# Expert weights of a two-block decoder loaded in runs of 16,384 bytes, one expert a unit, two units multiplied together

## The chip, the cores and the metric

The kernel is one program on one core of a Trainium2 chip. The metric is the device time of one execution in microseconds. Everything is float32; the matrix products of the experts run on TensorE as plain float32 matmuls. All weights come from HBM by DMAs that SyncE (SP) issues on one queue, and they pass through a ring of buffers in SBUF.

## The reference

Two blocks are computed one after the other on 256 tokens of width 1024. The first has two layers of a mixer (attention) and an expert-choice FFN; the second has one layer of another mixer and a hierarchical MoE. The change touches only how the weights of the two expert networks are fetched and multiplied:

```python
def expert_choice_ffn(h, w_router, w_gate, w_up, w_down):     # first block: 16 experts, D_EXPERT 1024
    cap = CAPACITY_FACTOR * S // N_EXPERTS                    # 32 tokens an expert
    aff = jax.nn.softmax(jnp.einsum('bsd,de->bse', h, w_router).astype(jnp.float32), axis=-1)
    gate, idx = lax.top_k(jnp.swapaxes(aff, 1, 2), cap)
    xe = h[bidx, idx]
    a = jnp.einsum('becd,edf->becf', xe, w_gate)
    u = jnp.einsum('becd,edf->becf', xe, w_up)
    ye = jnp.einsum('becf,efd->becd', jax.nn.silu(a) * u, w_down)
    return jnp.zeros_like(h).at[bidx, idx].add(gate[..., None].astype(h.dtype) * ye)

# second block: 4 groups of 8 experts, D_EXPERT_2 512, the two best of a group for each token
    hid = (jax.nn.silu(jnp.einsum('td,edf->tef', t, w_gate[gi]))
           * jnp.einsum('td,edf->tef', t, w_up[gi]) * combine[:, gi, :, None])
    out = out + jnp.einsum('tef,efd->td', hid, w_down[gi])
```

## The kernel before, in words

**Tiles and units.** Four experts (`TILE_E`) with 32 token slots each make one tile of 128 slots. The first block has two layers of four tiles, the second block eight tiles of experts of half the width. The weights of a tile come in units of 2 MB (128 partitions x 4096 float32, `UNIT`). A tile of the first block has 24 units: 8 of w_gate, 8 of w_up, 8 of w_down. A tile of the second block has 12: 4, 4 and 4. A unit holds the same rows of all four experts of the tile: for the first block row chunk c (128 rows of 1024), partition p taking row 128c+p of each expert, so that each partition gets four runs of 4096 bytes. In the second block partition p takes two rows of 512 of the eight rows 8p to 8p+7, again four runs of 4096 bytes. That makes 288 expert units in all, 604 MB of the 747 MB that are loaded.

**Buffers.** `RING` is 6 buffers; the first tile of each layer also uses four `spare` buffers in the arena (`FIRST_SLOTS`: units 0 to 11 go to buffers 9, 8, 7, 0, 1, 2, 3, 6, 4, 5, 9, 8; from unit 12 on the ring alone turns). So units 0 to 9 are loaded before the tile begins, unit 10 waits for unit 0 and unit 12 for unit 3. The second block has nine buffers in turn (`AHEAD2`), and unit n waits for unit n-9. SP issues the loads in a fixed order (`STREAMS`, `SEQ2`), and before each it waits until TensorE has finished with the unit that held the buffer. In layer 1 six loads of the second block's context weights (`CTX_LOADS`, 1 MB each in runs of 1024 bytes) stand in the same stream and take a ring buffer each; other work of the second block is put behind certain units on TensorE (`background`).

**TensorE.** `expert_tile` (L747) runs a tile. `tile_slots` (L743) gathers the tokens: 16 matmuls with rows of `hn_tok` as the stationary operand, giving `x_slots` [128 of D, chunk c, 128 slots]. L773 is the gate and up product: for each unit and each half of 512 columns four matmuls, one an expert, each with 32 columns of `x_slots` as the stationary operand and writing its own 32 partitions of the bank, so the four go to four different column groups of the array. `hid` (VectorE), its transposes (L787) and the down product L797 in the same form follow, then L807 adds the tile's result back to the tokens. Each float32 matmul shows as two records in the trace. A unit's mark (`unit u`) is what SP waits for.

**Layout.** In the first block `hn_tok` is natural and the weights are chunked by 128 rows; in the second ScalarE writes `hn_tok` permuted (L1932), so that the stationary rows of L743 are contiguous though partition p holds rows 8p to 8p+7 of the weights. `load_expert_unit` (L2791) builds the source of each load, `load` (L2785) issues it.

## Time and profile before

| | us |
|---|---|
| median of 3 runs | 2273.24 (2272.0 to 2279.18) |
| span of the profiled execution | 2272.4 |
| PE busy (matmul) | 1719.1 (76%) |
| DVE busy, ACT busy | 660.5 (29%), 554.7 (24%) |
| DMA, mean over the span | 330 GB/s |
| expert tiles of layer 0, by TensorE's rows | 289.84 to 744 |
| expert tiles of layer 1 | 1023.87 to 1505 |
| expert tiles of the second block | 1800.00 to 2256 |

The page cuts the span in 40 slices of 57 us; a digit is the busy share in tenths. PEclk is the clock that TensorE was granted, in tenths of 2.4 GHz. Rows of the timeline give start, duration, engine, line, operation and, in square brackets, how long the engine was idle before and what ended the wait. The page gives the span only; the median of the runs lies 0.8 us above it.

### The profile page before, as it was taken

To read this page: it belongs to the slowest core of one execution; us is meant where nothing else is said; L and a number is where in the kernel's file an instruction comes from. 1 tells how busy PE (TensorE), PEld (TensorE's weight loads), DVE (VectorE), ACT (ScalarE), POOL (GpSimd) and SP (SyncE) were. 2 spreads that over 40 slices of the span, in tenths; PEclk is the share of its full clock that TensorE was granted. 3 is DMA by queue.
4 is the path that set the end of the run, shared out by engine and by line. 5 is a ranking of instruction groups with operands and counts; after the bars stand their busy time and mean duration, and the time that the engine had idled before them with its cause. 6 is when DMAs were issued, how large, how long until landed. Compare 5 with 4: busy or idle time off the path is not lost.

```text
span 2272.4 us, 29204 instructions
## 1 busy us (share of the span) xinstructions
PE 1719.1 (76%) x12802; PEld 1052.0 (46%) x12802; DVE 660.5 (29%) x1074; ACT 554.7 (24%) x849; POOL 0.2 (0%) x4
## 2 busy tenths in 40 slices
PE   7989976565565999997676766669999976667665
PEld 6978932020111897892222323238988722222221
DVE  3477510000000447750250111037557400000001
ACT  3456300000000336630101221033444311010101
POOL 0000000000000000000000000000000000000000
PEclk9999998888788999998889889889999987777877
DMA  9732899999999963389999999983424999999996
GB/s 362 265 120 97 309 408 409 409 409 410 409 409 408 356 238 117 124 307 408 410 406 402 406 404 406 409 313 112 149 93 165 399 408 410 410 410 410 410 410 265
DMA packets 226975, 748.76 MB, mean 330 GB/s; under 512 B 6064, under 2 KB 18608, under 8 KB 226224
## 3 DMA queue, kind: packets, MB, share of 16 engines
q1 hardware_dynamic: 226864, 747.11, 84.5%
q8 instruction: 90, 1.47, 0.3%
q14 instruction: 21, 0.17, 0.0%
HBM read 746.04 MB, written 1.05 MB: 329 GB/s over the span
## 4 chain that ended last, share of the span: by engine, by line
DMA 40%; PE 39%; SPq 11%; ACT 4%; DVE 4%; issue 2%; DVEq 0%; ACTq 0%
PE bank L716 18%; DMA ring<-w_expert_down 16%; SPq L2785 11%; DMA ring<-w_expert_up 10%; DMA ring<-w_expert_gate 6%; PE bank L719 5%; PE bank L773 4%; DMA arena<-moe_w_up 3%; PE bank L797 2%; DMA ring<-moe_w_up 2%; PE bank L950 1%; PE bank L807 1%; DMA ring<-moe_w_down 1%; PE bank L970 1%; DMA ring<-ada_w 1%
## 5 line engine op out<-in xcount | busy, mean ns | idle before, releaser
L773 PE MATMUL bank<-ring,arena 128*32 128x512 f32 x2560 | 392.6, 746 | 235.0 <-DMA ring<-w_expert_up 110.2
L797 PE MATMUL bank<-ring,arena 128*32 128x512 f32 x1280 | 213.5, 802 | 167.8 <-DMA ring<-w_expert_down 132.7
L716 PE MATMUL bank<-arena_parts,ring_parts 128*128 128x256 f32 x1376 | 313.6, 283 | 2.4 <-DVE ring_parts L2430 1.6
L773 PEld LDWEIGHTS bank<-ring,arena 128*32 128x32 f32 x2560 | 79.3, 124 | 505.6 <-issue 162.8
L716 PEld LDWEIGHTS bank<-arena_parts,ring_parts 128*128 128x128 f32 x1376 | 232.7, 189 | 11.5 <-issue 3.1
L1495 ACT ACTIVATE arena<-bank 128x512 f32<-128x512 f32 (+1 forms) x150 | 76.0, 535 | 521.7 <-PE bank L787 252.5
L797 PEld LDWEIGHTS bank<-ring,arena 128*32 128x32 f32 x1280 | 40.7, 131 | 323.9 <-DMA ring<-w_expert_down 193.1
L2012 DVE TENSOR_TENSOR arena<-arena,bank 128x512 f32<-128x512 f32 x24 | 15.8, 685 | 592.4 <-PE bank L773 592.4
L716 PE MATMUL bank<-ring_parts 128*128 128x256 f32 x768 | 151.2, 287 | 11.7 <-DVE ring_parts L2430 5.3
L716 PE MATMUL bank<-hnT_parts,ring_parts 128*128 128x256 f32 x544 | 154.0, 283 | 0.0
L716 PEld LDWEIGHTS bank<-ring_parts 128*128 128x128 f32 x768 | 123.7, 192 | 14.8 <-issue 5.2
L1539 ACT ACTIVATE arena<-bank 128x512 f32<-128x512 f32 x32 | 17.4, 594 | 369.0 <-PE bank L797 369.0
L716 PEld LDWEIGHTS bank<-hnT_parts,ring_parts 128*128 128x128 f32 x544 | 103.6, 190 | 0.2 <-issue 0.2
L2417 DVE TENSOR_TENSOR hT<-hT,bank 128x512 f32<-128x512 f32 x32 | 22.0, 687 | 270.4 <-PE bank L807 270.3
L716 PE MATMUL bank<-arena_parts 128*128 128x256 f32 x352 | 98.9, 281 | 0.5 <-DVE hnT_parts L2175 0.4
L716 PE MATMUL bank<-hnT_parts,arena_parts 128*128 128x256 f32 x352 | 99.1, 281 | 0.0
L2164 DVE TENSOR_TENSOR ring_parts<-ring,arena_parts 128x2048 fp32r<-128x2048 f32 x30 | 68.7, 2291 | 82.8 <-ACT arena_parts L1598 82.8
L1797 ACT ACTIVATE ring_parts<-ring 128x2048 fp32r<-128x2048 f32 (+1 forms) x36 | 62.1, 1724 | 125.3 <-PE bank L716 100.0
L2430 DVE TENSOR_TENSOR ring_parts<-ring,ring_parts 128x2048 fp32r<-128x2048 f32 (+1 forms) x36 | 73.8, 2053 | 46.1 <-ACT ring_parts L1797 45.7
L773 PE MATMUL bank<-arena 128*32 128x512 f32 x512 | 65.2, 632 | 25.1 <-DMA arena<-moe_w_up 18.7
L2641 DVE SCALAR_TENSOR_TENSOR hT<-bank,arena,hT 128x256 f32<-128x256 f32 x72 | 31.3, 479 | 180.7 <-PE bank L807 169.5
L1598 ACT ACTIVATE arena_parts<-ring 128x2048 fp32r<-128x2048 f32 x30 | 57.4, 1915 | 101.5 <-PE bank L716 71.3
(353 smaller groups left out, 2384.4 us busy)
## 6 DMA issues: line engine op xcount, KB each, us to landing
ring<-w_expert_down SPq DMA_DIRECT2D x64, 2048.0 KB, 23.9
ring<-w_expert_up SPq DMA_DIRECT2D x60, 2048.0 KB, 23.7
ring<-w_expert_gate SPq DMA_DIRECT2D x56, 2048.0 KB, 23.6
ring<-w_in SPq DMA_DIRECT2D x34, 2048.0 KB, 11.0
ring<-moe_w_up SPq DMA_DIRECT2D x24, 2048.0 KB, 23.8
ring<-moe_w_gate SPq DMA_DIRECT2D x20, 2048.0 KB, 23.7
ring<-moe_w_down SPq DMA_DIRECT2D x16, 2048.0 KB, 23.8
arena<-moe_w_down SPq DMA_DIRECT2D x16, 2048.0 KB, 23.5
```

Of the source, the lines that this page charges most:

```text
L716: last = pe.matmul(out[:, n * S:(n + 1) * S], w[:, k, n * P:(n + 1) * P], x[:, k, :], start=first, stop=final)
L719: last = pe.matmul(out[:, n * JOB:(n + 1) * JOB], x[:, k, n * P:(n + 1) * P], w[:, k, :], start=first, stop=final)
L773: last = pe.matmul(banks[bank0 + f][32 * e:32 * e + 32, :], x_slots[:, c, 32 * e:32 * e + 32], w[:, k, e, f * 512:(f + 1) * 512], start=c ...
L797: last = pe.matmul(banks[4 + d][32 * e:32 * e + 32, :], hidT[:, f, 32 * e:32 * e + 32], w[:, e, d * 512:(d + 1) * 512], start=f == 0, stop ...
L807: last = pe.matmul(out[:, c * S:(c + 1) * S], y_sb[:, (2 * j + c) * P:(2 * j + c + 1) * P], spread_of(), start=True, stop=True)
L1495: act.activation(out, in_, ACT.Copy, scale=scale).then_inc(act_done, act_p.mark(step))
L1598: act.activation(high_room(i), job_weights(JOBS[i]), ACT.Copy)\
L1797: act.activation(w_high2[i % 2][:, 0:JOBS2[i][3], :], job2_weights(i), ACT.Copy)\
L2164: dve.tensor_tensor(job_weights(JOBS[i], ring_parts), w, high_room(i).bitcast(F32), ALU.subtract)\
L2430: dve.tensor_tensor(job2_weights(i, ring_parts), job2_weights(i), w_high2[i % 2][:, 0:JOBS2[i][3], :].bitcast(F32), ALU.subtract).then_inc ...
L2641: last = dve.scalar_tensor_tensor(h3[:, n, :], bank[:, c, :], ada[:, gate * DC + n, 0:1], h3[:, n, :], ALU.mult, ALU.add)
L2785: sp.dma_start(dst, src).then_inc(loaded(at), 16)
```

## The change

Each load of expert weights now reads one run of 16,384 bytes a partition. In the first block a unit is four of the eight rows that partition p owns (8p to 8p+7) of **one** expert's matrix; in the second block it is the whole matrix (8 rows of 512, or 4 rows of 1024) of one expert. The number of units (24 and 12 a tile), their size, the buffers and the order of loads by unit number stay. TensorE waits for two units, multiplies both (two experts, alternating), and marks both as done at the end of the pair. Because partition p now holds rows 8p to 8p+7, the stationary operand of the gather and of the transposes of `hid` is read with a step of 8 elements (4 for the second block's `hid`), and the copy of `hn_tok` on ScalarE in the second block becomes contiguous.

```diff
...
@@ -37,6 +37,9 @@
 
 TILE_E = 4
 SLOTS = P // TILE_E
+UNIT_E = 1
+UNIT_GROUPS = TILE_E // UNIT_E
+TAKEN = 2
 TILES1 = EXPERTS // TILE_E
 
 
...
+        def unit_counts(f_width):
+
+            rows = UNIT // f_width // UNIT_E
+            return DC * UNIT_GROUPS // rows, f_width // P * UNIT_GROUPS * D * UNIT_E // UNIT
+
         def slot2(at):
             return ring[at][:] if at < RING else spare2[at - RING]
 
@@ -740,16 +748,21 @@
                 for c in (2 * j, 2 * j + 1):
                     cols = slice((c % 2) * P, (c % 2 + 1) * P)
                     for half in range(TH):
-                        last = pe.matmul(out[:, cols], hn[:, half, c * P:(c + 1) * P], pick_of(half),
-                                         start=half == 0, stop=half == TH - 1)
+                        rows = hn[:, half, :].rearrange("t (q c) -> t c q", c=DC)[:, c, :]
+                        last = pe.matmul(out[:, cols], rows, pick_of(half), start=half == 0, stop=half == TH - 1)
                 last.then_inc(pe_done, pe_p.mark(f"{name} x{j}"))
 
             def expert_tile(name, prev, gather, loaded, spread_of, f_width, woven, place, behind=lambda u: None, back=None, turn=None):
 
                 fc = f_width // P
                 halves = f_width // 512
-                per_unit = 2 // halves
-                n_in = DC // per_unit
+                n_in, n_out = unit_counts(f_width)
+                in_rows, out_rows = DC * UNIT_GROUPS // n_in, fc * UNIT_GROUPS // n_out
+
+                def part(u, per):
+
+                    e0 = (u % UNIT_GROUPS) * UNIT_E
+                    return u // UNIT_GROUPS * per, range(e0, e0 + UNIT_E)
 
...
                 for which, bank0 in (("gate", 4), ("up", 6)):
-                    for n in range(n_in):
-                        u = n + (n_in if which == "up" else 0)
-                        loaded(u)
-                        w = place(u).rearrange("p (e k f) -> p k e f", k=per_unit, e=TILE_E)
-                        for k in range(per_unit):
-                            c = n * per_unit + k
-                            if which == "gate" and c % 2 == 0:
+                    u0 = n_in if which == "up" else 0
+                    for n in range(0, n_in, TAKEN):
+                        units = range(u0 + n, u0 + n + TAKEN)
+                        for u in units:
+                            loaded(u)
+                        c0, _ = part(n, in_rows)
+                        for k in range(in_rows):
+                            c = c0 + k
+                            if which == "gate" and n % UNIT_GROUPS == 0 and c % 2 == 0:
                                 if c in between:
                                     gather(c // 2 + 1)
                                 pe.wait_ge(act_done, act_at(f"{name} x{c // 2}", loops))
                             for f in range(halves):
-                                for e in range(TILE_E):
-                                    last = pe.matmul(banks[bank0 + f][32 * e:32 * e + 32, :],
-                                                     x_slots[:, c, 32 * e:32 * e + 32],
-                                                     w[:, k, e, f * 512:(f + 1) * 512],
-                                                     start=c == 0, stop=c == DC - 1)
-                        steps = [f"{name} unit {u}"] + ([f"{name} {which}"] if n == n_in - 1 else [])
-                        last.then_inc(pe_done, pe_p.mark(*steps))
-                        behind(u)
+                                for u in units:
+                                    w = place(u).rearrange("p (e k f) -> p k e f", k=in_rows, e=UNIT_E)
+                                    for i, e in enumerate(part(u - u0, in_rows)[1]):
+                                        last = pe.matmul(banks[bank0 + f][32 * e:32 * e + 32, :],
+                                                         x_slots[:, c, 32 * e:32 * e + 32],
+                                                         w[:, k, i, f * 512:(f + 1) * 512],
+                                                         start=c == 0, stop=c == DC - 1)
+                        steps = [f"{name} unit {u}" for u in units]
+                        last.then_inc(pe_done, pe_p.mark(*steps, *([f"{name} {which}"] if n == n_in - TAKEN else [])))
+                        for u in units:
+                            behind(u)
 
...
@@ -784,21 +802,27 @@
                 for j in range(fc // 4):
                     out = to_act(f"{name} hidT{j}")
                     for f in range(4):
-                        last = pe.transpose(out[:, f * P:(f + 1) * P], hid[:, (4 * j + f) * P:(4 * j + f + 1) * P],
-                                            ident)
+                        cols = hid[:, 0:f_width].rearrange("p (q c) -> p c q", c=fc)[:, 4 * j + f, :]
+                        last = pe.transpose(out[:, f * P:(f + 1) * P], cols, ident)
                     last.then_inc(pe_done, pe_p.mark(f"{name} hidT{j}"))
...
+                for n in range(0, n_out, TAKEN):
+                    units = range(2 * n_in + n, 2 * n_in + n + TAKEN)
+                    for u in units:
+                        loaded(u)
+                    f0, _ = part(n, out_rows)
+                    for k in range(out_rows):
+                        f = f0 + k
+                        for d in range(2):
+                            for u in units:
+                                w = place(u).rearrange("p (e k d) -> p k e d", k=out_rows, e=UNIT_E)
+                                for i, e in enumerate(part(u - 2 * n_in, out_rows)[1]):
+                                    last = pe.matmul(banks[4 + d][32 * e:32 * e + 32, :], hidT[:, f, 32 * e:32 * e + 32],
+                                                     w[:, k, i, d * 512:(d + 1) * 512], start=f == 0, stop=f == fc - 1)
...
@@ -1927,9 +1951,8 @@
             def token_rows(j):
                 half, c0 = j // 2, 4 * (j % 2)
 
-                place = hn_tok[:, half, :].rearrange("t (k c q) -> t c q k", k=DC, c=DC)[:, c0:c0 + 4]
                 act.wait_ge(pe_done, pe_at(f"hn_tok2 {j}"))
-                act.activation(place, banks[4 + j][:].rearrange("t (c q k) -> t c q k", c=4, k=DC), ACT.Copy,
+                act.activation(hn_tok[:, half, c0 * P:(c0 + 4) * P], banks[4 + j][:], ACT.Copy,
                                scale=t_inv[:, half:half + 1]).then_inc(act_done, act_p.mark(f"hn_tok2 {j}"))
 
             act.wait_ge(dve_done, dve_at("m norm inv"))
@@ -2790,21 +2813,14 @@
 
             def load_expert_unit(at, u, gate, up, down, t, f_width, slot=slot, loaded=lambda at: unit_loaded[at]):
 
-                per_unit = 2 // (f_width // 512)
-                n_in = DC // per_unit
-                if u < 2 * n_in:
-                    c = (u % n_in) * per_unit
-                    src = gate if u < n_in else up
-                    src = src[bass.ds(t * TILE_E, TILE_E), :, :]
-                    if per_unit == 1:
-                        src = src[:, c * P:(c + 1) * P, :].rearrange("e p f -> p e f")
-                    else:
-                        src = src.rearrange("e (p c) f -> p e (c f)", c=DC)[:, :, c * f_width:(c + per_unit) * f_width]
-                    load(at, slot(at).rearrange("p (e x) -> p e x", e=TILE_E), src, loaded)
-                else:
-                    f = u - 2 * n_in
-                    src = down[bass.ds(t * TILE_E, TILE_E), f * P:(f + 1) * P, :]
-                    load(at, slot(at).rearrange("p (e d) -> p e d", e=TILE_E), src.rearrange("e p d -> p e d"), loaded)
+                n_in, n_out = unit_counts(f_width)
+                src = gate if u < n_in else up if u < 2 * n_in else down
+                n = u % n_in if u < 2 * n_in else u - 2 * n_in
+                e0 = t * TILE_E + n % UNIT_GROUPS * UNIT_E
+                cols = UNIT // UNIT_E
+                rows = src[bass.ds(e0, UNIT_E), :, :].rearrange("e (p r) x -> p e (r x)", p=P)
+                first = n // UNIT_GROUPS * cols
+                load(at, slot(at).rearrange("p (e x) -> p e x", e=UNIT_E), rows[:, :, first:first + cols], loaded)
 
             ctx_starts = [3 * KD, 3 * KD + JOB, KD, KD + JOB, 2 * KD, 2 * KD + JOB]
             for layer in range(LAYERS):
```

What the change does to the order on the engines, at three places. In the rows, "bank4" and "bank5" are the two halves of 512 columns, "ring4" is ring buffer 4, and "32x512" one matmul of one expert; the words in brackets are the semaphores waited for.

TensorE, the first units of the down product of layer 0's first tile, before:

```order
L797 MATMUL bank4<-ring4,arena 32x512 [waits unit_loaded_4,scalar_steps_done]
L797 MATMUL bank4<-ring4,arena 32x512 x3
L797 MATMUL bank5<-ring4,arena 32x512 x4
L797 MATMUL bank4<-ring5,arena 32x512 [waits unit_loaded_5]
L797 MATMUL bank4<-ring5,arena 32x512 x3
L797 MATMUL bank5<-ring5,arena 32x512 x4
```

and in the changed kernel:

```order
L820 MATMUL bank4<-ring4,arena 32x512 [waits unit_loaded_5,unit_loaded_4,scalar_steps_done]
L820 MATMUL bank4<-ring5,arena 32x512
L820 MATMUL bank5<-ring4,arena 32x512
L820 MATMUL bank5<-ring5,arena 32x512
L820 MATMUL bank4<-ring4,arena 32x512
L820 MATMUL bank4<-ring5,arena 32x512
L820 MATMUL bank5<-ring4,arena 32x512
L820 MATMUL bank5<-ring5,arena 32x512
```

Before, four matmuls in a row are four experts of one buffer; now two in a row are two experts of two buffers, and the next two go to the same two experts again. The number of matmuls for two units, 16, is the same.

TensorE, the start of layer 0's first tile (L743 is the gather, L773 the gate product), before:

```order
L743 MATMUL bank1<-arena 128x128 [waits scalar_steps_done,vector_steps_done]
L743 MATMUL bank1<-arena 128x128 x3
L743 MATMUL bank0<-arena 128x128 [waits scalar_steps_done]
L743 MATMUL bank0<-arena 128x128 x3
L773 MATMUL bank4<-arena 32x512 [waits scalar_steps_done,unit_loaded_9]
L773 MATMUL bank4<-arena 32x512 x3
L773 MATMUL bank5<-arena 32x512 x4
```

and in the changed kernel, where L752 and L790 are those two:

```order
L752 MATMUL bank1<-arena 128x128 [waits scalar_steps_done,vector_steps_done]
L752 MATMUL bank1<-arena 128x128 x3
L752 MATMUL bank0<-arena 128x128 [waits scalar_steps_done]
L752 MATMUL bank0<-arena 128x128 x3
L790 MATMUL bank4<-arena 32x512 [waits scalar_steps_done,unit_loaded_8,unit_loaded_9]
L790 MATMUL bank4<-arena 32x512
L790 MATMUL bank5<-arena 32x512 x2
L790 MATMUL bank4<-arena 32x512 x2
L790 MATMUL bank5<-arena 32x512 x2
L752 MATMUL bank1<-arena 128x128 [waits scalar_steps_done]
```

The first mark, for which SP waits with the load of unit 10, stood behind 8 matmuls; now it stands behind 16 and a third gather.

SP, the loads of layer 1's second tile around the first context loads ("128x4x1024" is four runs of 1024 elements a partition), before:

```order
L2785 DMA ring<-w_expert_gate 128x4x1024 [waits tensor_steps_done] x8
L2785 DMA ring<-w_expert_up 128x4x1024 [waits tensor_steps_done] x4
L2785 DMA ring<-w_in 128x8x256 [waits tensor_steps_done]
L2785 DMA ring<-w_expert_up 128x4x1024 [waits tensor_steps_done] x4
L2785 DMA ring<-w_expert_down 128x4x1024 [waits tensor_steps_done] x3
```

and in the changed kernel:

```order
L2808 DMA ring<-w_expert_gate 128x4096 [waits tensor_steps_done] x8
L2808 DMA ring<-w_expert_up 128x4096 [waits tensor_steps_done] x4
L2808 DMA ring<-w_in 128x8x256 [waits tensor_steps_done]
L2808 DMA ring<-w_expert_up 128x4096 [waits tensor_steps_done] x4
L2808 DMA ring<-w_expert_down 128x4096 [waits tensor_steps_done] x3
```

The loads stand in the same order; only the shape of each and the moment at which its buffer is released differ.

## Rows read from the trace of the kernel before

**Rows 1.** The page: DMA share and rate by slice; the chain by engine

```profile
DMA  9732899999999963389999999983424999999996
GB/s 362 265 120 97 309 408 409 409 409 410 409 409 408 356 238 117 124 307 408 410 406 402 406 404 406 409 313 112 149 93 165 399 408 410 410 410 410 410 410 265
DMA 40%; PE 39%; SPq 11%; ACT 4%; DVE 4%; issue 2%; DVEq 0%; ACTq 0%
```

**Rows 2.** Windows: busy time by engine, granted clock, DMA share and rate

```profile
core 0: us, PE busy (x) PEld busy (x) DVE busy (x) ACT busy (x) POOL busy (x), PEclk, DMA share, GB/s
20.00:60.00 40.00, 39.47 (x456) 38.00 (x457) 19.96 (x19) 13.79 (x13) 0.00 (x0) 0.96 1.05 386
350.00:370.00 20.00, 10.55 (x64) 2.03 (x64) 0.00 (x0) 0.00 (x0) 0.00 (x0) 0.83 1.03 409
800.00:850.00 50.00, 50.00 (x426) 50.00 (x424) 22.19 (x14) 19.30 (x18) 0.00 (x0) 1.00 0.70 252
1900.00:2100.00 200.00, 136.42 (x810) 43.25 (x810) 13.76 (x33) 22.97 (x49) 0.00 (x0) 0.76 1.03 410
```

**Rows 3.** Timeline of TensorE, units before and behind hid, layer 0's first tile

```profile
329.57 1.92 PE L773 MATMUL bank<-ring,arena 128*32 128x512 f32 x16 [1.77 <-DMA ring<-w_expert_up]
...
334.78 1.92 PE L797 MATMUL bank<-ring,arena 128*32 128x512 f32 x16 [0.78 <-ACT arena L1495]
...
344.93 3.35 PE L797 MATMUL bank<-ring,arena 128*32 128x512 f32 x16 [2.62 <-DMA ring<-w_expert_down]
350.05 1.92 PE L797 MATMUL bank<-ring,arena 128*32 128x512 f32 x16 [1.77 <-DMA ring<-w_expert_down]
```

**Rows 4.** Timeline of layer 1, two units either side of the hgrn_lb load

```profile
1091.94 3.60 PE L797 MATMUL bank<-ring,arena 128*32 128x512 f32 x16 [3.20 <-DMA ring<-w_expert_down]
1099.55 3.21 PE L797 MATMUL bank<-ring,arena 128*32 128x512 f32 x16 [4.01 <-DMA ring<-w_expert_down]
```

**Rows 5.** Timeline: three units run together, and one round's weight loads

```profile
302.18 5.36 PE L773 MATMUL bank<-ring,arena 128*32 128x512 f32 x48
...
303.06 0.13 PEld L773 LDWEIGHTS bank<-ring,arena 128*32 128x32 f32 x4 [0.30 <-issue]
```

**Rows 6.** Timeline: products on two column groups (L991) and on one (L807)

```profile
150.66 2.81 PE L991 MATMUL bank<-arena 128*64 128x256 f32 x24
...
373.19 3.94 PE L807 MATMUL bank<-arena 128*128 128x256 f32 x16 [0.76 <-issue]
```

**Rows 7.** Timeline of TensorE, start of layer 0's first tile, and a later gather

```profile
289.84 1.92 PE L773 MATMUL bank<-arena 128*32 128x512 f32 x16
...
292.81 1.84 PE L1171 MATMUL bank<-cst,arena 16*128 16x1 f32 x16
...
376.97 3.73 PE L743 MATMUL bank<-arena 128*128 128x128 f32 x32
```

**Rows 8.** Timeline of TensorE, end of layer 0 and the next DMA wait

```profile
740.47 3.55 PE L797 MATMUL bank<-ring,arena 128*32 128x512 f32 x16 [3.23 <-DMA ring<-w_expert_down]
...
756.94 3.20 PE L1040 MATMUL bank<-ring,arena 128*32 128x128 f32 x64 [2.64 <-DMA ring<-ada_w]
```

**Rows 9.** Window from layer 1's tile 2 to tile 3, context products (L719) alone

```profile
core 0: us, PE busy (x) PEld busy (x), PEclk, DMA share, GB/s
1253.97:1387.28 133.31, 17.26 (x144) 16.67 (x144) 0.86 1.03 404
```

**Rows 10.** Second block: first loads behind the gate, first tiles, last unit

```profile
1802.23 6.22 SPq L2785 DMA_DIRECT2D arena<-moe_w_down  x3
...
1800.00 1.93 PE L773 MATMUL bank<-arena 128*32 128x512 f32 x16 [1.10 <-DVE arena L2729]
...
1832.43 1.92 PE L773 MATMUL bank<-ring,arena 128*32 128x512 f32 x16
...
2252.18 3.64 PE L797 MATMUL bank<-ring,arena 128*32 128x512 f32 x16 [1.39 <-DMA ring<-moe_w_down]
```

**Rows 11.** ScalarE copies: min/median/max ns; permuted target (L1932), plain (L1775)

```profile
L1932 ACT ACTIVATE arena<-bank,small x4: 1108/1129/1156, 1789.2 to 1794.1; 128x512 f32<-128x512 f32 x4
L1775 ACT ACTIVATE arena<-bank,small x8: 679/684/689, 277.5 to 1014.2; 128x512 f32<-128x512 f32 x8
```

15 lines of the change are left out of this document (4 added, 11 removed).

## Prediction, made before the changed kernel ran

> **What bounds the kernel now.** I read the slices first [rows 1]: in the three expert stretches (slices 5 to 13, 18 to 26 and 31 to 39) the DMA digit is 9 and the rate stands at 404 to 410 GB/s, elsewhere it falls to 100 to 300. The chain gives DMA 40% and SP 11% beside PE 39%. The windows [rows 2] say the same: a DMA share of 1.03 at 409 to 410 GB/s while TensorE is busy for only 10.55 of 20 us. Then the timeline [rows 3]: two units arrive 5.12 us apart (344.93, 350.05), TensorE takes 1.92 or 3.35 us for one and waits for the DMA again. So an expert tile of 24 units lasts 24 x 5.12 = 122.9 us because of the load rate, and TensorE has slack. Two things decide: what the rate becomes, and whether TensorE still has slack.
>
> **The load rate.** Runs of 2048 bytes move at 386 GB/s in 20 to 60 us, runs of 4096 at 409.6 (2,097,152 bytes in 5.12 us) [rows 2, 3]. With 16 engines a run takes 2048 x 16 / 386 = 84.9 ns and 4096 x 16 / 409.6 = 160.0 ns, so 2048 bytes more cost 75.1 ns and each run some 9.8 ns beside its bytes. A run of 16384 bytes would take 160.0 + 6 x 75.1 = 610.6 ns, 429 GB/s, and a unit 4.89 us: 0.23 us less. The trace has one longer run to check with: the 1 MB load of hgrn_lb (8192 bytes a run) stands between two units that are 1099.55 - 1091.94 = 7.61 us apart [rows 4], so it took 7.61 - 5.12 = 2.49 us, 421 GB/s, where the fit gives 422. Bounds: nothing gained (409.6), what 8192 bytes showed (421, a unit of 4.98 us), and the fit; the far end, no cost beside the bytes, is 436 GB/s, 4.81 us. I take the fit, since it met the one row that tests it.
>
> The Trainium skill (DMA: Bandwidth & Descriptors, Why small descriptors are slow) puts the cost of a descriptor at about 3 cycles of its bus beside one cycle for 32 bytes: 128 + 3 against 512 + 3, so at best 1.7% from 4096 to 16384, a unit of 5.03 us. From 2048 to 4096 the same rule gives 2.3%, and the trace shows 6.1%; so the sum goes by the rows.
>
> **TensorE's work doubles.** Four matmuls to four column groups run side by side: three units take 5.36 us, 1.73 each, in rounds of four, 0.43 us apart, with the weight loads of the next round hidden [rows 5]. In the changed order only two experts alternate, so a third matmul must wait for the first. L991 is that case with 256 columns: two column groups, 24 records in 2.81 us, twelve rounds of 0.21 us and an end; L807, one group, takes 3.94 us for 16 [rows 6]. So a pair takes 16 rounds of 0.43 us, 6.9 us (before 3.5), against 9.8 us in which the DMA brings the next. Per tile of a first-block layer: 12 x 6.9 = 83 us, 3.3 us for hid (331.49 to 334.78 [rows 3]) and 8.3 us for the tile's end (from 0.77 us ahead of L807 at 373.19 to the gather's end at 380.70 [rows 6, 7]), 95 against 117 of loading. Second block: six pairs, 41.5 us; its first tile took 1832.43 - 1800.00 = 32.4 us with all its weights there [rows 10], of which 12 x 1.73 = 20.8 were units and 11.6 the rest (13.5 in every other tile); so 53 to 55 us against 12 x 4.89 = 58.7. TensorE stays behind the DMA in both, by little in the second block.
>
> **Layer 0.** The buffers are released later. Before, unit 0 is done 2 us after 289.84. Now: first pair with a gather of 1.2 us, 297.9; the small products behind it 3.2 us [rows 7]; then pairs at 308.0, 316.1 (gather), 323.0, 329.9, 336.8, 343.7. Unit 18 needs the buffer of unit 12, which falls free at 343.7 instead of long before. With 2 us from issue to landing beside the data (my estimate) it lands at 350.6, not 344.9: 5.6 us late. From there the DMA is full again: 77 units x 0.23 = 17.7 us gained. The last unit lands 12 us earlier; its pair costs 6.9 instead of 3.55 us [rows 8], of which 2.6 us are covered by the wait for ada_w at 756.94 [rows 8]. Layer 0: -12 + 0.8 = **-11 us**.
>
> **Layer 1.** The same late start, 5 us. But here the DMA's background products lie on TensorE. Tile 2 lasts from 1253.97 to 1387.28, 133.3 us, and its context products alone are 17.26 us [rows 9]; with the small ones I count some 26 us, in tile 1 some 30. TensorE then needs 95 + 26 to 30 = 121 to 125 us, the DMA 117 + 2 or 3 context loads of 3 us = 123 to 126. With two of six buffers held by the pair and one by a context load, the two can't overlap fully. I take no gain in tile 1, 3 us lost in tile 2, 5 gained in tile 3 (16 us of background), 1 in the rest of tile 0, and 3 lost at the end, where the last pair is bare: 5 - 1 + 0 + 3 - 5 + 3 = **+5 us**.
>
> **Second block.** The first loads behind the gate are issued at 1802.23 [rows 10], when unit 0 is done; now at 1800 + 6.9 + 2.3 (gathers) = 1809.2: 7 us lost. Then 87 units x 0.23 = 20 us gained, and the last pair 6.9 for 3.64 us: 3.3 lost. **-10 us**.
>
> **Strided weight loads.** The stationary operands of the gather and of hid's transposes are now read with a step of 8 (or 4) elements. No row shows TensorE reading so. Below: nothing. Nearest: ScalarE's permuted copy, 1129 ns against 684 for the plain one [rows 11], 1.65 times. A gather is 32 records in 3.73 us [rows 7], bound by its weight loads; 1.65 times is 2.4 us a tile, 2 times 3.7. I take 2.4. In layer 0 and the second block it hides in the slack except at the starts and ends (1 and 3 us); in layer 1, where there is none, 4 us. **+8 us.** The plain copies on ScalarE save 4 x 0.45 us, but VectorE's routing ends later there (its L2729 releases the first product at 1800.00 [rows 10]): nothing. The Trainium skill (SBUF — State Buffer, Specifications (TRN2)) says that each cross to a new 16-byte line costs, and a step of 8 float32 is 32 bytes: it speaks for a price here, and the ScalarE rows agree.
>
> SP issues the same loads in the same order; with a quarter of the runs its issue can only be shorter, and it waits for buffers anyway. VectorE's and ScalarE's work is unchanged.
>
> **Sum.** -11 + 5 - 10 + 8 = -8 us on the span of 2272.4, which lies 0.8 us below the median: 2273.2 - 8 = **2265 us**, 0.4% faster. Ends: no stride cost 2257; two times, 2269; a unit of 4.98 us, 0.09 x about 200 bound units = +18, 2283.
>
> **The rivals.**
> 1. *The stride costs nothing* (TensorE reads a stationary column at a step as fast): 2257. Against it ScalarE's rows.
> 2. *Runs above 4096 bytes gain less.* Only one load of 8192 bytes speaks for the fit, and none of 16384. By that row alone 2283; by the skill's rule above the unit of 5.03 us gives 2293.
> 3. *The rate doesn't rise at all*, so the change doesn't do what it says: layer 0 +7 (the start, no gain), layer 1 +19 (start, tiles and end), second block +10, stride 3: 2312. The engines' share of 1.03 at 409 speaks for engine-bound runs, thus against it.
> 4. *TensorE becomes the bound, slower than before.* The clock falls between units now: 0.83 and 0.76 in the expert windows, 1.00 where TensorE is never idle [rows 2]; a unit after an idle stretch of 2.6 us took 3.35 us, at 1.2 GHz for most of it, the next after 1.77 us took 1.92 [rows 3]. After the change a pair is 6.9 us of work and 2.9 us of idleness, so the fall may come in each pair. One fall costs up to 3.4 us and makes the pair 10.3 us, more than the 9.8 us of the DMA; with no idle time left the clock should hold in the next. It decides from the point where a pair with all its stalls passes 9.8 us. If half the pairs cost 10.3 us, the expert stretches go at 5.0 us a unit and layer 1's tiles lose 5 us each: about 2290. If two column groups don't bring the clock back at all, a pair takes 13.7 us and the three stretches 48 x 13.7 = 660, 700 and 760 us: about 2970. No row shows a long stretch of two groups.
>
> **Chances.** Forecast 0.33 (2258 to 2272), rival 1 0.22, rival 2 0.17, rival 3 0.10, rival 4 mild 0.10 and severe 0.04, more gained than the fit says (no cost beside the bytes) 0.04, 2245. A measurement of this kernel can tell 0.3%, 6.8 us. Faster by more: half of the forecast, nearly all of rival 1, the last: 0.43. Within: 0.22. Slower: 0.35. The range of 8 in 10 leaves out the severe case, part of rival 3 and what lies under 2248: 2248 to 2312.
>
> **What would show it.** The DMA slices in the expert stretches at 425 to 430 GB/s (right), or 410 (rival 3) or 415 to 421 (rival 2). Records of a pair over 6.9 us and a PEclk near 1.0; 13.7 us would be rival 4. Gap of DMA rate just behind 1800 and unit 18 at 350. Gather records in the tile's end: 3.7, or 6.1 us with the stride's cost. In layer 1 tiles 1 and 2 of 126 to 136 us. The forecast is wrong if tile 2 of layer 0 isn't 117 to 118 us, or if TensorE no longer waits for the DMA in it.

## The result

The changed kernel took 2298.31 us (median of 4 runs, 2294.76 to 2303.07) beside 2273.88 us for the kernel before in the same session (2272.0 to 2279.18): **1.0103 times, with a 95% interval of 1.0084 to 1.0122, so 1.0% slower**. The profiled execution has a span of 2301.3 us (before 2272.4). Forecast were 2265 us and a gain of 0.4%.

The page of the changed kernel: granted clock, DMA share and rate in 40 slices, and the chain by engine (before: [rows 1]).

```profile
PEclk9999999999999999999999999999999999999999
DMA  9733789999999852569999899993332989999996
GB/s 363 256 120 106 310 339 428 423 428 424 428 421 415 319 217 74 214 267 375 423 402 369 361 377 377 400 380 110 111 112 102 372 369 427 428 428 428 429 429 253
...
PE 65%; DMA 24%; DVE 5%; ACT 4%; issue 2%; SPq 1%; DVEq 0%; ACTq 0%
```

The first and last expert stretch (slices 7 to 12, 34 to 39) now run at 421 to 429 GB/s instead of 409 to 410. The middle one, layer 1, falls to 361 to 402 in slices 21 to 26, below the 402 to 409 of before. TensorE holds 65% of the chain instead of 39%.

Windows of the changed kernel: one in layer 0, the third expert tile of layer 1, and one in the second block; columns as in [rows 2].

```profile
core 0: us, PE busy (x) PEld busy (x) DVE busy (x) ACT busy (x) POOL busy (x), PEclk, DMA share, GB/s
350.00:370.00 20.00, 15.40 (x68) 4.38 (x70) 0.00 (x0) 0.09 (x1) 0.00 (x0) 0.96 1.01 432
1265.14:1410.36 145.22, 126.79 (x618) 58.23 (x618) 19.82 (x23) 29.95 (x36) 0.00 (x0) 0.95 0.88 367
1920.00:2120.00 200.00, 179.02 (x824) 77.02 (x820) 17.73 (x43) 27.99 (x57) 0.00 (x0) 0.97 1.01 428
```

The same third tile of layer 1 in the kernel before, from the end of its second tile to that of its third:

```profile
1246.50:1379.82 133.32, 92.19 (x619) 43.14 (x619) 19.81 (x23) 30.20 (x36) 0.00 (x0) 0.86 1.03 406
```

The same 619 or so TensorE records are busy for 126.79 us instead of 92.19. In these windows of layer 0 and the second block the DMA share is still 1.01, so the loads set the pace there; in layer 1's third tile it is 0.88, and neither engine is full.

Timelines of the changed kernel's TensorE (a record is one line of the trace; a pair is the 32 records of two units): three pairs of layer 0's first tile; the gather behind it; pairs and background work in layer 1's third tile; the last pair of all.

```profile
350.14 7.06 PE L820 MATMUL bank<-ring,arena 128*32 128x512 f32 x32 [0.72 <-ACT arena L1519]
358.93 7.06 PE L820 MATMUL bank<-ring,arena 128*32 128x512 f32 x32 [1.73 <-DMA ring<-w_expert_down]
368.72 8.64 PE L820 MATMUL bank<-ring,arena 128*32 128x512 f32 x32 [2.73 <-DMA ring<-w_expert_down]
...
390.19 7.67 PE L752 MATMUL bank<-arena 128*128 128x128 f32 x32
...
1345.52 8.35 PE L790 MATMUL bank<-ring,arena 128*32 128x512 f32 x32 [3.79 <-DMA ring<-w_expert_up]
1353.79 1.16 PE L908 MATMUL bank<-arena 128*128 128x128 f32 x8
1355.33 7.06 PE L790 MATMUL bank<-ring,arena 128*32 128x512 f32 x32 [0.38 <-DMA ring<-w_expert_up]
1363.82 1.16 PE L806 MATMUL bank<-cst,arena 128*128 128x128 f32 x8 [1.43 <-DVE arena L2035]
1369.62 9.94 PE L820 MATMUL bank<-ring,arena 128*32 128x512 f32 x32 [4.64 <-DMA ring<-w_expert_down]
...
2277.71 7.06 PE L820 MATMUL bank<-ring,arena 128*32 128x512 f32 x32 [2.79 <-DMA ring<-moe_w_down]
```

A pair takes 7.06 us (1.92 or 3.35 us a unit before [rows 3]); behind idle times some take 8.35 to 9.94, others don't. The gather takes 7.67 us (3.73 before [rows 7]). In layer 1 TensorE waits up to 5.2 us for loads although the DMA has idle time too: the loads had waited for buffers. SP's longest waits in the third tile, for the marks behind the context products, in the changed kernel and in the one before (us in total, times, longest):

```profile
SPq L2808 <- PE bank L727: 59.9, 3, 24.2
```

```profile
SPq L2785 <- PE bank L719: 32.2, 3, 12.9
```

**Where the time went.** I cut each profiled span at the first expert product and at the first spread-back record (L807 before, L831 after) of the last tile of each expert stretch. Microseconds; the last column is the whole run against before, by medians.

| kernel | layer 0 | layer 1 | second block | rest | span | ratio |
|---|---|---|---|---|---|---|
| before | 455.0 | 481.8 | 456.6 | 879.0 | 2272.4 | 1 |
| changed | 451.6 | 514.5 | 450.3 | 884.9 | 2301.3 | 1.0103 |
| stride alone (e1) | 454.2 | 483.6 | 455.8 | 883.9 | 2277.5 | 1.0018 |
| changed, contiguous tokens (e2) | 447.5 | 494.7 | 447.7 | 881.7 | 2271.6 | 0.9984 |
| 8192 bytes, single units (e3) | 447.2 | 477.4 | 447.2 | 884.2 | 2256.0 | 0.9926 |
| before in pairs (e4) | 456.2 | 490.6 | 461.3 | 881.0 | 2289.1 | 1.0064 |
| 8192 bytes, pairs, four groups (e5) | 445.2 | 480.5 | 448.6 | 884.4 | 2258.7 | 0.9928 |
| e3 with contiguous tokens (e6) | 445.4 | 476.5 | 446.0 | 879.6 | 2247.5 | 0.9877 |
| 16384 bytes, one group (e7) | 575.0 | 677.9 | 642.2 | 880.2 | 2775.3 | one run |
| 16384 bytes, four units together (e8) | 489.4 | 586.3 | 457.7 | 885.7 | 2419.1 | 1.064 |
| changed, light context (e9) | 450.8 | 494.0 | 449.8 | 882.2 | 2276.8 | one run |
| before, light context (e10) | 455.4 | 482.0 | 456.4 | 877.9 | 2271.7 | one run |
| e3, pairs waited for and released together (e11) | 450.3 | 494.1 | 452.7 | 880.5 | 2277.6 | 1.0031 |
| e3, pairs released together only (e12) | 448.8 | 479.7 | 448.9 | 889.5 | 2266.9 | 0.9942 |

The rest, which no edit aims at, scatters by some 5 us either way, so I read no difference of that size in a single column. The runs come from several sessions, in which the kernel before had medians of 2273.9 to 2276.9 us, so 3 us between two runs of different sessions mean nothing either. Of the changed kernel's +28.9 us, layer 1 has +32.7; the other two stretches gain 9.7 together, and the rest has +5.9.

The same cut at the end of each tile shows more. The first tile of each stretch, for which ten of 24 units (nine of 12 in the second block) are loaded ahead, lost 11.1, 13.7 and 16.5 us, 41.3 together. The later tiles of layer 0 and the second block gained 14.5 and 22.8; those of layer 1 lost another 19.0. So the loss has two places: the three first tiles, and the rest of layer 1.

### The profile page after: what moved, and what is told of

The parts are those of the page before. It is cut to its first block, busy times and chain, and to the rows that moved or that the text cites. A ratio compares the mean times of both kernels' runs of the same rounds, so it can differ in the third digit from the quotient of the medians.

```text
span 2301.3 us, 29232 instructions
## 1 busy us (share of the span) xinstructions
PE 2069.9 (90%) x12802; PEld 1250.7 (54%) x12802; DVE 660.5 (29%) x1074; ACT 553.4 (24%) x849; POOL 0.2 (0%) x4
## 4 chain that ended last, share of the span: by engine, by line
PE 65%; DMA 24%; DVE 5%; ACT 4%; issue 2%; SPq 1%; DVEq 0%; ACTq 0%
PE bank L724 18%; PE bank L790 17%; PE bank L820 8%; DMA ring<-w_expert_down 8%; DMA ring<-w_expert_up 7%; PE bank L752 5%; PE bank L727 5%; DMA ring<-moe_w_down 4%; DMA arena<-moe_w_down 3%; PE bank L831 2%; DMA ring<-w_expert_gate 2%; PE bank L974 1%; PE bank L994 1%; PE bank L735 1%; PE bank L1041 1%
## 5 line engine op out<-in xcount | busy, mean ns | idle before, releaser
L790 PE MATMUL bank<-ring,arena 128*32 128x512 f32 x2560 | 573.9, 616 | 54.5 <-DMA ring<-w_expert_up 35.2
L820 PE MATMUL bank<-ring,arena 128*32 128x512 f32 x1280 | 325.8, 618 | 62.9 <-DMA ring<-w_expert_down 45.3
L790 PEld LDWEIGHTS bank<-ring,arena 128*32 128x32 f32 x2560 | 157.7, 113 | 407.6 <-issue 404.6
L820 PEld LDWEIGHTS bank<-ring,arena 128*32 128x32 f32 x1280 | 89.4, 113 | 264.6 <-issue 254.6
L790 PE MATMUL bank<-arena 128*32 128x512 f32 x512 | 138.5, 603 | 0.5 <-DMA arena<-moe_w_up 0.4
L752 PEld LDWEIGHTS bank<-arena 128*128 128x128 f32 x512 | 124.7, 334 | 20.6 <-issue 20.2
L752 PE MATMUL bank<-arena 128*128 128x128 f32 (+1 forms) x512 | 128.9, 406 | 3.0 <-issue 3.0
L820 PE MATMUL bank<-arena 128*32 128x512 f32 x256 | 89.2, 641 | 12.4 <-DMA arena<-moe_w_down 8.4
L1821 ACT ACTIVATE ring_parts<-ring 128x2048 fp32r<-128x2048 f32 (+1 forms) x36 | 62.0, 1724 | 125.8 <-PE bank L724 101.3
## 6 DMA issues: line engine op xcount, KB each, us to landing
ring<-w_expert_gate SPq DMA_DIRECT2D x56, 2048.0 KB, 16.7
```

Of the source, the lines that this page charges most:

```text
L752: last = pe.matmul(out[:, cols], rows, pick_of(half), start=half == 0, stop=half == TH - 1)
L790: last = pe.matmul(banks[bank0 + f][32 * e:32 * e + 32, :], x_slots[:, c, 32 * e:32 * e + 32], w[:, k, i, f * 512:(f + 1) * 512], start=c ...
L820: last = pe.matmul(banks[4 + d][32 * e:32 * e + 32, :], hidT[:, f, 32 * e:32 * e + 32], w[:, k, i, d * 512:(d + 1) * 512], start=f == 0, s ...
L1821: act.activation(w_high2[i % 2][:, 0:JOBS2[i][3], :], job2_weights(i), ACT.Copy)\
```

## The experiments

Two theories stood at the outset. **G**: the products go to two column groups instead of four, so TensorE takes twice as long for a unit and has no time left for the background work of layer 1. **B**: buffers are held and released in pairs, so the ring starves. A third, **S**, gave the loss to the strided stationary reads.

### e1: the stride alone

```diff
-UNIT_E = 1
+UNIT_E = 4
-TAKEN = 2
+TAKEN = 1
```

> The row layout of the change (a partition holds neighbouring rows, so the stationary tokens and the hidden rows are read with a stride) with the loads of before: four experts a unit, runs of 4096 bytes, four column groups, every unit released by itself. It prices the stride alone. Theory G (the loss comes from TensorE's products going in two column groups instead of four: a unit then takes 3.5 us of TensorE at full clock instead of 1.9) and theory B (the loss comes from holding and releasing the buffers two by two) expect the same here: the gather of a tile takes 7.7 us instead of 3.7, of which the idle time of TensorE between units hides most in the tiles that it does not open; 2274 + 5 to + 15, likeliest 2282. Theory S (the stride is most of the loss) expects 2295 or more.

Measured 2279.65 us, 1.0018 (1.0006 to 1.0030): **+4 us**, just under the 5 to 15 expected and far from the 20 of S. It prices both strided reads, of the gather and of the hidden rows; e2 and e6 below give back the gather's alone.

### e2: the changed kernel with tokens read contiguously

```diff
-rows = hn[:, half, :].rearrange("t (q c) -> t c q", c=DC)[:, c, :]
+rows = hn[:, half, c * P:(c + 1) * P]
```

and at both places where ScalarE writes the tokens:

```diff
-act.activation(hn_tok[:, half, c0 * P:(c0 + 4) * P], bank, ACT.Copy, ...)
+place = hn_tok[:, half, :].rearrange("t (k c q) -> t c q k", k=DC, c=DC)[:, c0:c0 + 4]
+act.activation(place, bank.rearrange("t (c q k) -> t c q k", c=4, k=DC), ACT.Copy, ...)
```

> The changed kernel with the tokens written in permuted order by ScalarE (as the second block did before, 1129 ns instead of 684 a piece), so that TensorE's gather reads them contiguously; the reads of the hidden rows stay strided. It should bring the gather back from 7.7 to 3.7 us. Theory G, by which TensorE has little idle time left: up to 4 us in each of 16 tiles where it is the bound, 2298 - 15 to - 30, likeliest 2280. Theory B: only the four or five gathers that nothing hides, 2298 - 5 to - 10, likeliest 2290. Theory S: back below before, 2265.

Measured 2272.15 us, 0.9984 (0.9974 to 0.9993): **26 us less than the changed kernel**, within what G expected, beyond B, and short of S. One line, in the changed kernel and then in this one (minimum, median and maximum in ns):

```profile
L752 PEld LDWEIGHTS bank<-arena x512: 312/335/340, 287.9 to 2243.3; 128*128 128x128 f32 x171
```

```profile
L751 PEld LDWEIGHTS bank<-arena x512: 186/192/338, 287.6 to 2209.8; 128*128 128x128 f32 x171
```

The stride costs 4 us in e1 and 26 here. Layer 1 alone gives back 19.8 us, 5 a tile for 3.9 us less of TensorE: there TensorE's time counts in full, and that a later release adds the rest is likely but not shown. Without the gather's stride the changed kernel is level with before, so the stride could be called the loss; but so could the pairs (e3) or four fifths of it the context products (e9). Each gives back the same slack.

### e3: two experts a unit, one unit at a time

```diff
-UNIT_E = 1
+UNIT_E = 2
-TAKEN = 2
+TAKEN = 1
```

> Two experts a unit, runs of 8192 bytes, one unit taken at a time and released by itself: the two column groups of the changed kernel without its pairs. Strides as in the change. Theory G: TensorE takes 3.5 us a unit as in the changed kernel, and layer 1 with its background products stays long, 2290 to 2300. Theory B: buffers come free one by one, the load runs at 420 GB/s, and layer 1's loss is gone: 2260 to 2270. Both: warm units of 3.5 us each (16 or 17 of 32 records in 3.5 us).

Measured 2258.93 us, 0.9926 (0.9910 to 0.9943): **16 us faster than before**, 1 us below the range of B and far from G. Timeline of its TensorE in layer 0, and a window there:

```profile
524.40 3.63 PE L790 MATMUL bank<-ring,arena 128*32 128x512 f32 x16 [1.34 <-DMA ring<-w_expert_gate]
529.37 3.63 PE L790 MATMUL bank<-ring,arena 128*32 128x512 f32 x16 [1.35 <-DMA ring<-w_expert_gate]
```

```profile
350.00:370.00 20.00, 14.51 (x64) 3.38 (x64) 0.00 (x0) 0.00 (x0) 0.00 (x0) 1.00 1.01 421
```

A unit of two groups takes 3.63 us alone, just half a pair of the changed kernel, and layer 1 takes 477.4 us instead of 514.5. Two column groups a unit by themselves therefore cost nothing that the faster loads don't repay; neighbouring units use different groups here, and where both are there they overlap (last section).

### e4: the kernel before, in pairs

```diff
+if n % 2 == 0:
+    loaded(u)
+    loaded(u + 1)
...
+if n % 2:
+    steps = [f"{name} unit {u - 1}", f"{name} unit {u}"] + ...
+    last.then_inc(pe_done, pe_p.mark(*steps))
+    behind(u - 1)
+    behind(u)
```

> The kernel before with its own loads and four column groups, but units waited for, marked done and released two by two, with the work behind both after the second. It prices the pairs alone. Theory G: TensorE needs 2 x 1.9 to 2 x 3.4 us of a 10.2 us pair, the releases come a few us late and six buffers bear it: 2274 + 0 to + 10. Theory B: the ring starves behind the background products of layer 1 as in the changed kernel, which gives layer 1 alone + 20 to + 30: 2295 to 2305.

Measured 2290.72 us, 1.0064 (1.0047 to 1.0081): +15 us, between the two theories, 8.8 of it in layer 1. Pairs cost with four groups as well, but less than half of what layer 1 lost.

### e5: 8192 bytes in pairs, four groups

```diff
-UNIT_E = 1
+UNIT_E = 2
```

> Two experts a unit in runs of 8192 bytes, two units taken together: four column groups again, buffers held and released two by two, strides as in the change. With the single 8192-byte units on record at 2259, this adds the pairs and takes the two-group products away. If both halves of the loss are real (theory G + B): the first tiles, whose weights are all there, are as short as with four groups (second block's start to its first tile's end 30 to 32 us, against 34.1 with two groups and single units and 43.1 in the changed kernel), but the ring is released late as with the pairs of 4096-byte runs, which cost 15 us: 2259 + 15 - 8 = 2266. Theory G alone: 2250. Theory B alone: 2274.

Measured 2259.94 us, 0.9928 (0.9912 to 0.9945): 6 us under the 2266 expected, 10 over G alone and 14 under B alone, and level with e3. With two column groups and no pairs, 2259; with pairs and four groups, 2260; with both, and longer runs, the changed kernel has 2298. **Either one alone leaves the longer runs their gain; both together take it away.** Neither theory alone holds. Whether the two prices merely add up is open: pairs alone cost 15 us in e4, and no run has 8192-byte runs with four groups and single units.

### e6: e3 with contiguous tokens

The edits of e2 and e3 together.

> Two experts a unit in runs of 8192 bytes, units taken and released singly, and the tokens written in permuted order by ScalarE so that the gather reads them contiguously. The contiguous gather was worth 26 us in the changed kernel, where TensorE had little idle time, and its stride cost 4 us with the loads of before, where it had much. Here TensorE waits for the DMA 1.34 us in each 4.97 us unit. Theory G (the price of the stride depends on the slack): between the two, 2259 - 5 to - 12, likeliest 2251. If the 26 us belonged to the pairs: 2259 - 4 = 2255.

Measured 2248.8 us, 0.9877 (0.9857 to 0.9896): 1.2% faster than before, the fastest of all. The gather's stride was worth 10 us here, between e1's 4 and e2's 26, as expected if its price follows TensorE's slack.

### e7: one expert a unit, one column group

```diff
-TAKEN = 2
+TAKEN = 1
```

> The loads of the change (one expert a unit, 16384-byte runs), each unit taken and released by itself, so that TensorE's products go to one column group at a time. Theory G (time of a product follows the number of column groups in flight): 16 records of 128x512 in 6.9 us, more than the 4.89 us of a load; TensorE is the bound and an expert tile of a layer takes 24 x 6.9 + 12 = 178 us; in all about 2259 + 8 x 58 + 8 x 27 = 2940. If two groups already run one behind the other and only four overlap: 3.5 us a unit, tiles of 118 us, 2255 to 2265.

Measured 2777.66 us (one run). The timeline of layer 0's second tile:

```profile
499.42 29.93 PE L790 MATMUL bank<-ring,arena 128*32 128x512 f32 x89
```

89 records in 29.93 us are 5.38 us for 16, with no wait: slower than four or two groups, less than the 6.9 expected for one product strictly behind the other. The sum with 5.38 gives an expert tile of 24 x 5.38 + 12 = 141 us; measured 143.5.

### e8: one expert a unit, four units together

```diff
-TAKEN = 2
+TAKEN = 4
```

> The loads of the change (one expert a unit, 16384-byte runs), but four units taken together, so that the products go in four column groups again, while four of the six buffers are held until the last product of the four. Strides as in the change. It sets the two causes against each other. Theory G mostly (TensorE's doubled time): TensorE needs 7 to 9 us of the 19.6 us that four units take to load; the second block's first tile is short again (30 us) and layer 1's tile 2 is under 140: 2260 to 2275. Theory B mostly (held buffers): only two loads can be in flight while TensorE works and the DMA stands idle once per four units, in layer 1 behind the background above all: 2300 to 2330.

Measured 2422.38 us, 1.064 (1.0622 to 1.0658), beyond the worse expectation of both. Its TensorE in layer 0, and the window of layer 1's third tile:

```profile
531.68 7.07 PE L790 MATMUL bank<-ring,arena 128*32 128x512 f32 x64 [1.39 <-DMA ring<-w_expert_gate]
553.77 8.88 PE L790 MATMUL bank<-ring,arena 128*32 128x512 f32 x64 [15.02 <-DMA ring<-w_expert_gate]
```

```profile
1324.17:1508.94 184.77, 93.96 (x618) 50.17 (x619) 19.81 (x23) 29.96 (x36) 0.00 (x0) 0.73 0.72 296
```

TensorE is busy for 93.96 of 184.77 us and the DMA for 72%: both wait for each other, since four of six buffers are held. In layer 1 it lost 105 us against before and in layer 0 34, both with six buffers; in the second block, with nine, 1. So holding buffers costs by how few are left. TensorE's granted clock of 0.73 in this window has its part in the time of the four units (7.07 us, or 8.88 behind 15.02 us of idleness), which no run separates.

### e9 and e10: less background work

The two correcting passes of layer 1's context products are left out, in the changed kernel and in the kernel before:

```diff
-passes_ = ((high, src_high), (high, src_low), (low, src_high))
+passes_ = ((high, src_high), (high, src_low), (low, src_high))[:n_passes]
```

with n_passes 1 in the context products and 3 elsewhere.

> The changed kernel with the context products of layer 1 in one pass instead of three (high times high part only; the two correcting passes are left out, so its output differs a little): in tile 2 of layer 1 TensorE has 17.3 - 5.8 = 11.5 us less work, in all six jobs about 35 us less. The loads and their order are unchanged. Theory G (in layer 1 TensorE's doubled products and the background together pass what the loads leave): tile 2 falls from 145.2 to 134 to 138 us, and the whole by 12 to 25 us, to about 2280. If the loss of layer 1 comes from the loads (their order, the extra context loads, the held buffers alone): tile 2 stays at 143 to 145, the whole at 2295 or more.

> The kernel before with the context products of layer 1 in one pass instead of three (the two correcting passes are left out, so its output differs a little): the same TensorE work taken away as in the changed kernel, where it gave 20 us and 12.4 us in tile 2. Theory G (before had slack there, TensorE busy 92 of 133 us in tile 2): tile 2 falls by 0 to 3 us from 133.3 and the whole by 0 to 8 us, 2267 to 2275. If background products on TensorE delay the loads there as well: tile 2 at 125 to 129, the whole at 2255 to 2262.

Measured 2278.58 and 2273.49 us (one run each). The third tile of layer 1 in the two:

```profile
1258.41:1391.24 132.83, 113.42 (x522) 47.57 (x522) 19.82 (x23) 29.96 (x36) 0.00 (x0) 0.96 0.96 398
```

```profile
1247.34:1379.07 131.73, 90.36 (x523) 33.96 (x523) 19.80 (x23) 30.19 (x36) 0.00 (x0) 0.76 1.03 407
```

The changed kernel's tile falls from 145.2 to 132.8 us, a little below the 134 to 138 expected, its layer 1 by 20.5; before, the tile falls by 1.6 and the layer not at all. The loads and their order are unchanged in each, so 20.5 of the 32.7 us that layer 1 lost hang on TensorE's background work, which was hidden before and no longer is. The other 12 us are no matter of the context products: with these light in both kernels, layer 1's four tiles take 105.8, 131.4, 132.8 and 124.1 us in the changed kernel and 92.8, 131.7, 131.7 and 125.8 in the one before, so what remains stands in the first tile, which begins with ten units there, so that at first TensorE sets the pace and not the loads.

### e11 and e12: waiting and releasing apart

e3 with both units of a pair waited for, marked and released together and the work behind both last (e11), and with the marks, release and work alone moved (e12). The order of the products stays that of e3, one unit wholly ahead of the next.

```diff
+if n % 2 == 0:
+    loaded(u0 + n)
+    loaded(u0 + n + 1)
...
+if n % 2:
+    steps = [f"{name} unit {u}" for u in (u0 + n - 1, u0 + n)]
```

> The single 8192-byte units at 2259 (two column groups at a time) with one thing changed: both units of a pair are waited for before the first product, marked done and released together after the second, with the work behind both after that; the order of the products stays. Theory GB (the loss comes from the two together: a pair of some 7 us in two groups, whose buffers come free only at its end, behind which the background work also lies): most of the loss is back, 2259 + 20 to + 35, likeliest 2285, layer 1's tile 2 at 138 to 145 instead of 131.3. Rival R (pairs cost nothing by themselves at this run length, as four groups and pairs at 2260 suggest; the loss of the changed kernel is in its order of products, which are slower when several units are there: 5.8 us a pair against 4.4): 2260 to 2266, tile 2 at 131 to 134.

> The same, but each unit is waited for by itself, so that the first unit's products run while the second is still on its way; only the mark, the release and the work behind come after the second. It parts waiting from releasing. Theory GB with the release as the cause: the first unit's buffer comes free one unit (4.97 us) late, the pair's end is as early as with single units, so 2259 + 5 to + 12. If the waiting is the cause (the pair starts when its second unit is there and then lasts 7 us): 2259 + 0 to + 5. Rival R: 2259 to 2262.

Measured 2281.54 us, 1.0031 (1.0021 to 1.0040), and 2263.87 us, 0.9942 (0.9926 to 0.9959): e11 within what GB expected and against R, e12 at the border of its two readings. Timeline of e11's TensorE in layer 0, and windows of the first 3.3 us and the last 3.2 us of its first row:

```profile
541.15 7.05 PE L791 MATMUL bank<-ring,arena 128*32 128x512 f32 x32 [2.97 <-DMA ring<-w_expert_up]
551.10 7.05 PE L791 MATMUL bank<-ring,arena 128*32 128x512 f32 x32 [2.90 <-DMA ring<-w_expert_up]
...
581.29 5.38 PE L823 MATMUL bank<-ring,arena 128*32 128x512 f32 x32 [0.73 <-ACT arena L1523]
```

```profile
541.10:544.40 3.30, 3.25 (x9) 0.93 (x11) 0.00 (x0) 0.00 (x0) 0.00 (x0) 0.53 1.00 415
545.00:548.20 3.20, 3.20 (x24) 0.75 (x16) 0.00 (x0) 0.00 (x0) 0.00 (x0) 1.00 1.00 417
```

**The pair costs 23 us with two groups (e11 - e3): 5 from the later release, 18 from waiting for the second unit.** While TensorE waits for the second, the first can't be worked on; the whole pair then lies behind the second's landing. 16.7 of the 23 us are in layer 1. The clock belongs to the 18 us too: the pairs of 7.05 us, behind 2.9 us of idleness, begin at a granted clock of 0.53, near the lower level of 1.2 GHz, and end at 1.00, and a pair that begins at the full 2.4 GHz takes 5.38 us. In e3, which waits 1.34 us between units, the clock was 1.00 over 200 us of the second block (1900 to 2100), in e11 0.91. How much of the 18 us is the clock, no run separates.

From e11 to the changed kernel 17 us more remain, 20.4 in layer 1; 19.4 stand in the three first tiles. Two things lie between: runs of 16384 bytes, and, with one expert a unit, the products of a pair, which alternate between two column groups where e11's go to two groups and then to the other two. The longer runs should have helped (422 to 429 GB/s), and at the full clock a pair takes 7.06 us in the changed kernel and 5.38 in e11. So the products' groups and order are the likely cause (below); no run changed them alone.

## Why the prediction failed

- **The load rate: right.** Forecast 429 GB/s for 16384 bytes and 422 for 8192; measured 428 to 429 and 421 to 422. The fit to two run lengths held. The rival by which runs above 4096 bytes gain less, and the descriptor rule of the Trainium skill (DMA: Bandwidth & Descriptors, Why small descriptors are slow) with its unit of 5.03 us, are out: a unit took about 4.9 us (9.79 us a pair, 358.93 to 368.72).
- **TensorE's pair: right.** Forecast 6.9 us, measured 7.06. (The working's 1.73 us a unit is four rounds of 0.43; its row of 5.36 us for three units gives 1.79, too little to matter.) The clock's fall, the mild form of rival 4, came in some 26 of the 144 pairs, mostly at 1.7 us each (8.64 us behind 2.73 us of idleness). In layer 0 and the second block the next wait took it up where there was one; what the nine such pairs of layer 1 cost, no run separates. The severe form did not come; the clock was 0.95 to 0.97 in the windows above.
- **Layer 0: -11 forecast, -3.4 measured** (-1.3 with a first product 2.1 us later, behind strided gathers). Unit 19 was awaited until 358.9, not 355.5 as the working implies (the first pair's mark came at 302, not 297.9, and the loads behind it with it), and the tile ended 13 us later than before, where the working gives 10. The three other tiles took 357.1 instead of 371.6 us, 14.5 gained of 17.7; the last had 120.4 us.
- **Layer 1: +5 and +4 for the stride forecast, +32.7 measured. This is the step that failed.** It has 24 of the 37 us by which the spans miss the forecast. The first tile lost 13.7 us (forecast 4, or 7 with the bare last pair, which a cut at tile ends shows already here), the second 4.4 (0), the third 11.9 (3), the fourth 2.7 (forecast 5 gained and 3 lost at its end). The prediction had the ingredients: 121 to 125 us of TensorE work against 123 to 126 of loading, and two buffers held by the pair. But it then *took* 0, 3 and 5 us where it should have followed the ring through the tile. In the third tile TensorE had 126.8 us of work and the DMA about as much (a share of 0.88), and coupled through six buffers in lumps of two they took 145.2. In the first tile it counted the loads' late start as in layer 0 and nothing more; there TensorE sets the pace at first, and the tile gave back 1.6 us without the background work and 9.3 with single units of 8192 bytes. The runs show what each ingredient gives back: less background work 20 us (e9); single units and shorter runs 37 (e3); contiguous tokens 20 (e2). They overlap, since each gives back the same slack.
- **The stride: +8 forecast.** A gather takes 2.06 times as long (7.67 us for 3.73), above the 1.65 taken from ScalarE and at the 2 named as the bound. In the kernel before that is worth 4 us (e1), in the changed one 26 (e2). The mis-sized term is less the factor than the assumption that idle time hides it: TensorE had too little in layer 1. The Trainium skill's rule on 16-byte lines (SBUF — State Buffer, Specifications (TRN2)) pointed the right way; the weight load's 335 ns against 192 agrees with it.
- **Second block: -10 forecast, -6.3 measured.** The first tile took 43.1 us from first product to its end, 26.6 before: 16.5 lost, where the step had 7. With all weights there, TensorE is the bound, and the forecast counted only the first unit's later release. Behind it 22.8 us were gained, more than the 20 - 3.3, so the two misses nearly cancel; that the stretch came out near its forecast (-7 with its 3 us of stride) is luck.
- **The rivals.** None was it. By number the 2293 of rival 2 and the 2290 of rival 4 lie nearest, but the rate rose as forecast. Rival 4 laid such a loss to the clock; e9 and e3 show most of layer 1's to come with the background work and the pairs, beside which the clock fell in a sixth of the pairs. Its two times are also added wrongly: 0.11 us for each of 164 units and 5 us for each of layer 1's four tiles are 38 us, thus about 2303, and the severe form's stretches with the 879 us of the rest come to about 3000, not 2970. The measured time lies within the range of 2248 to 2312, on the side given a chance of 0.35, which is no credit to the working, since its terms for layer 1 were 24 us short.

## What to carry to other kernels

Longer runs do raise the load rate, but how a unit is cut also sets how many column groups work at once and how many buffers are held until the last product. Where all weights are there, it is TensorE's time for them that counts, however fast the loads. Where two engines' work in a stretch comes within a few per cent of each other, don't take the larger as the stretch's time: follow the buffers through it, background work included. Here two experts a unit, each unit released by itself, kept most of the rate (422 of 429 GB/s) without holding pairs, and turning a strided stationary read into a permuted write of ScalarE cost nothing that shows.

## What the runs showed of the hardware

- **Column groups.** 16 records of 128x512, float32, took 1.92 us in four groups [rows 3], 3.53 to 3.63 in two, 5.38 in one group at a time (e7).
- **Units of different groups overlap when both are there.** In e3 each unit uses two groups and the next unit the other two. Its timeline in the second block, a stretch that catches up and then a unit that waited:

```profile
2078.39 7.14 PE L790 MATMUL bank<-ring,arena 128*32 128x512 f32 x48
2086.45 3.63 PE L790 MATMUL bank<-ring,arena 128*32 128x512 f32 x16 [0.92 <-DMA ring<-moe_w_up]
```

And e6 at the start of the second block, where the weights are there:

```profile
1795.07 0.62 PE L789 MATMUL bank<-ring,arena 128*32 128x512 f32 x2
1795.48 0.60 PE L789 MATMUL bank<-arena 128*32 128x512 f32 x2
1795.52 0.60 PE L789 MATMUL bank<-ring,arena 128*32 128x512 f32 x2
1795.91 0.60 PE L789 MATMUL bank<-arena 128*32 128x512 f32 x2
```

Three units in 7.14 us are 2.4 each, against 3.63 alone. In e6 records of two units, one reading from the arena and the other from the ring, start in turn, though the program has all of one ahead of the other. Where its weights are all there, the second block's first eight units took 17.6 us without gathers in e6 (4.4 a pair), 23.1 in the changed kernel (5.8 a pair) and 14.0 before (3.5). e11 took 17.7 us for them, like e6. So units whose neighbours use the other two groups went faster than pairs that alternate within two groups, which fits the 17 us between e11 and the changed kernel.
- **Strided stationary reads.** A 128x128 float32 weight load takes 335 ns with a step of 8 elements and 192 without. The rule in the Trainium skill (TensorE: Matmul & The Clock Gate, LDWEIGHTS (loading the stationary operand)) has the column count set the time; with the same 128 columns in both, these rows differ from it. The hidden rows' weight loads, also strided, went from 142 to 194 ns only.
- **Issuing a load.** In the kernel before, with four runs a partition, a load's issue holds SP for 4.9 us (median), about as long as the load itself takes; in the changed kernel, with one run, for 0.33 to 0.43 us, shorter as forecast. Before and changed (minimum, median and maximum in ns):

```profile
L2785 SPq DMA_DIRECT2D ring<-w_expert_down x64: 367/4917/10139, 311.0 to 1479.2; - x64
```

```profile
L2808 SPq DMA_DIRECT2D ring<-w_expert_down x64: 327/428/10896, 331.3 to 1509.8; - x64
```

With two runs a partition (e3) the median is 0.37 us. It is no fixed price of the four runs: in e4, whose loads have them too but fall due in pairs, the median of all expert loads of the first block is 1.04 us. The chain's SP share falls from 11% [rows 1] to 1%; that this gained time by itself isn't shown.
- **The clock** was 1.00 in e3's window of 350 to 370 us, where TensorE idles 0.97 to 1.35 us between units of 3.63, and 0.83 in the same window before [rows 2], with idle times of 1.75 to 3.20.
